# One stage for the two long convolutions of a layer, the short convolution inside its linear, and filter spectra over even and odd tokens

## What is computed

```python
def hyena_filter_spectra(z, window, w1, b1, w2, b2, w3, b3, freq):
    ...                                   # a small network of the position gives h
    h = (h @ c(w3) + c(b3)).reshape(L, HY_ORDER, 2, HY_WIDTH) * window[:, None, None, :]
    fwd, bwd = h[:, :, 0], h[:, :, 1]
    f = jnp.concatenate([fwd, zeros, bwd[1:][::-1]], axis=0)
    f = f / (jnp.sum(jnp.abs(f), axis=0, keepdims=True) + EPS)
    return jnp.fft.rfft(f, axis=0)

def hyena_mixer(u, conv_w, spec, skip):
    u = short_conv(u, conv_w)             # three taps over tokens, 1536 channels
    v, x1, x2 = jnp.split(u, 3, axis=-1)
    z = x1 * long_conv(v, spec[:, 0], skip[0])
    return x2 * long_conv(z, spec[:, 1], skip[1])
```

## Time and profile before

| | us |
|---|---|
| median of three runs | 3400.32 |
| lowest, highest | 3399.54, 3415.02 |
| the profiled execution | 3400.13 |
| its span in the trace | 3398.3 |
| TensorE busy | 2941.6 (87%) |
| VectorE busy | 2106.3 (62%) |
| ScalarE busy | 1482.0 (44%) |
| mean granted TensorE clock, share of full speed | 0.913 |

### The profile page before, as it was taken

The page is one execution under the profiler, slowest core; times in us unless marked ns, Lnnn a source line. Parts: engine busy times, 40 slices in busy tenths (PEclk is TensorE's granted clock), DMA queues, the critical chain, the costliest instruction groups (busy, mean ns, idle before and its releaser), DMA issues. The chain is left out here.

```text
span 3398.3 us, 44680 instructions
## 1 busy us (share of the span) xinstructions
PE 2941.6 (87%) x18175; PEld 2619.8 (77%) x18175; DVE 2106.3 (62%) x2152; ACT 1482.0 (44%) x1353; POOL 40.0 (1%) x65
## 2 busy tenths in 40 slices
PE   5999974699999999999967696898999686899899
PEld 4799973578888888888843584898899584899898
DVE  5555557378888888888846453555555454555554
ACT  3443432156766776676622023343434023343432
POOL 0000000000000000000000000000000000000000
PEclk8899986689999999999979886899999886899999
DMA  5255520089999999999941240344355230354352
GB/s 164 73 178 184 161 88 1 0 300 347 363 333 347 363 333 344 365 333 342 367 135 75 64 124 13 121 165 132 104 185 164 75 113 25 112 161 137 100 186 100
DMA packets 364966, 618.36 MB, mean 182 GB/s; under 512 B 16670, under 2 KB 201092, under 8 KB 363536
## 3 DMA queue, kind: packets, MB, share of 16 engines
q1 hardware_dynamic: 363656, 610.87, 52.3%
q10 hardware_dynamic: 1162, 5.36, 0.4%
HBM read 610.94 MB, written 5.24 MB: 181 GB/s over the span
## 5 line engine op out<-in xcount | busy, mean ns | idle before, releaser
L345 DVE TENSOR_TENSOR slots_low<-slots,w_hi 128x2048 fp32r<-128x2048 f32 (+2 forms) x241 | 542.1, 2253 | 579.7 <-ACT w_hi L334 579.7
L334 ACT ACTIVATE w_hi<-slots 128x2048 fp32r<-128x2048 f32 (+2 forms) x241 | 451.7, 1878 | 585.0 <-PE ps L426 263.1
L1166 DVE TENSOR_TENSOR slots_low<-slots,w_hi 128x2048 fp32r<-128x2048 f32 x224 | 504.0, 2285 | 70.7 <-ACT w_hi L1118 70.7
L426 PE MATMUL ps<-x_hi,w_hi 128*128 128x256 f32 x1488 | 438.3, 295 | 120.1 <-DVE x_lo L497 40.1
L426 PE MATMUL ps<-x_lo,w_hi 128*128 128x256 f32 x1488 | 432.9, 291 | 0.0
L426 PE MATMUL ps<-x_hi,slots_low 128*128 128x256 f32 x1488 | 432.4, 291 | 0.0
L1118 ACT ACTIVATE w_hi<-slots 128x2048 fp32r<-128x2048 f32 x224 | 415.8, 1908 | 1.1 <-DMA slots<-in_moe_w_up_dram 1.0
L426 PEld LDWEIGHTS ps<-x_hi,w_hi 128*128 128x128 f32 x1488 | 298.2, 200 | 126.5 <-issue 89.9
L1050 PE MATMUL ps<-slots_low,x_hi 128*128 128x512 f32 x896 | 349.6, 390 | 0.0
L426 PEld LDWEIGHTS ps<-x_lo,w_hi 128*128 128x128 f32 x1488 | 298.4, 201 | 0.5
L426 PEld LDWEIGHTS ps<-x_hi,slots_low 128*128 128x128 f32 x1488 | 297.8, 200 | 0.0
(11 more groups left out here) (517 smaller groups left out, 5782.9 us busy)
## 6 DMA issues: line engine op xcount, KB each, us to landing
slots<-in_moe_w_gate_dram SPq DMA_DIRECT2D x112, 1024.0 KB, 5.1
slots<-in_moe_w_up_dram SPq DMA_DIRECT2D x112, 1024.0 KB, 5.2
slots<-in_moe_w_down_dram SPq DMA_DIRECT2D x112, 1024.0 KB, 4.9
slots<-in_mlp_w_dram SPq DMA_DIRECT2D x64, 1024.0 KB, 5.3
slots<-in_w_in_dram SPq DMA_DIRECT2D x54, 1024.0 KB, 5.3
slots<-in_ffn_w_gate_dram SPq DMA_DIRECT2D x14, 1024.0 KB, 5.0
slots<-in_ffn_w_up_dram SPq DMA_DIRECT2D x14, 1024.0 KB, 5.0
slots<-in_ffn_w_down_dram SPq DMA_DIRECT2D x14, 1024.0 KB, 4.9
```

Source lines behind the costliest of these rows:

```text
L334: act.activation(w_hi[:, s.buffer, 0:s.kt * s.cols], slots[:, s.slot, 0:s.kt * s.cols], ACT.Copy).then_inc(w_hi_done, 1)
L345: dve.tensor_tensor(slots_low[:, s.slot, 0:n], slots[:, s.slot, 0:n], w_hi[:, s.buffer, 0:n].bitcast(F32), ALU.subtract).then_inc(w_lo_don ...
L426: mm = pe.matmul(b[:, t * T:(t + 1) * T], w, xx[:, k, :], **flags)
L1166: dve.tensor_tensor(low[i % NS], raw[i % NS], his[i % R].bitcast(F32), ALU.subtract).then_inc(lo_done, 1)
```

## The change

Three places are changed.

- **Short convolution.** The stage of its own is gone. Functions hung on the linear's hooks compute the taps of slab j-2 at step j, and those of slabs 4 and 5 at step 6, the last: the first tap on ScalarE (two instructions per slab), the other two on VectorE (four per slab).
- **Long convolutions.** One stage holds both. Tokens are taken as even and odd ones, as the new layout of the `dft` constant demands; the upper frequency half is stored in falling order. VectorE starts multiplying as soon as the first of the four forward results is there, GpSimd combines each part as soon as its two factors are, and TensorE transforms back part by part, accumulating in four banks at once. Skip and gate follow per m, and the second convolution turns tile m when it is done.
- **Spectra.** Filters are made for even and odd tokens. One product instead of two gives each of four half results, and GpSimd, in `join`, forms the spectra of both halves as their sums and differences. The sizes are computed from the sum p and the difference q of the filters, as max(|p|, |q|): |p| on ScalarE, |q| and the maximum on VectorE. The order of VectorE is now `size(i)`, `window(i+1)`, `scale(i)`, `store(i)`, `mix(i+1)`. ScalarE waits for the joined spectra of unit i before it sends them and goes on to unit i+1.

```diff
-    c["hy_window"] = np.ascontiguousarray(win.reshape(TT, P, 512).transpose(1, 0, 2)).reshape(P, -1)
-    k = np.arange(T)
+    c["hy_window"] = np.ascontiguousarray(win.reshape(P, TT, 512)).reshape(P, -1)
+    k = np.concatenate([i, T - 1 - i])
...
-    c["dft"] = np.ascontiguousarray(cs.reshape(2, TT, P, T).transpose(2, 1, 0, 3)).astype(np.float32).reshape(P, -1)
+    c["dft"] = np.ascontiguousarray(cs.reshape(2, P, TT, T).transpose(1, 2, 0, 3)).astype(np.float32).reshape(P, -1)
...
@@ spectra, tensor @@
-                                    pe.matmul(bank(2 * d + t), h2[:, l, t * P:(t + 1) * P], w3s[l][...],
+                                    pe.matmul(bank(2 * d + t), h2[:, l, t:T:2], w3s[l][...],
...
                         def transform(i, n):
-                            s, k = n // 2, n % 2
-                            for t in range(TT):
-                                mm = pe.matmul(bank(4 + n), dft[:, t, s, k * P:(k + 1) * P], pq[:, s, t, :], start=(t == 0), stop=(t == TT - 1))
-                            mm.then_inc(transformed, 1)
+                            s, t = n // 2, n % 2
+                            pe.matmul(bank(4 + n), dft[:, t, s, 0:P], pq[:, s, t, :], start=True, stop=True).then_inc(transformed, 1)
                         make(0)
                         for i in range(N):
-                            pe.wait_ge(absd, 2 * i + 2)
-                            if i:
-                                pe.wait_ge(outed, 4 * i)
-                            for n in range(4):
-                                mm = pe.matmul(bank(4), ones[:, :], ab[:, n // 2, n % 2, :], start=(n == 0), stop=(n == 3))
-                            mm.then_inc(summed, 1)
                             if i + 1 < N:
                                 make(i + 1)
                             pe.wait_ge(mixed, 2 * i + 2)
+                            if i:
+                                pe.wait_ge(outed, 4 * i)
                             for n in (1, 2, 3):
                                 transform(i, n)
+                            pe.wait_ge(added, i + 1)
+                            for t in range(TT):
+                                mm = pe.matmul(bank(4), ones[:, :], ab[:, t, :], start=(t == 0), stop=(t == TT - 1))
+                            mm.then_inc(summed, 1)
                             pe.wait_ge(shifted, i + 1)
                             transform(i, 0)
@@ spectra, vector @@
+                        def size(i):
+                            dve.wait_ge(mixed, 2 * i + 2)
+                            dve.scalar_tensor_tensor(out=flat(fb[:, 1]), in0=flat(pq[:, 1]), scalar=-1.0, in1=flat(pq[:, 1]),
+                                                     op0=ALU.mult, op1=ALU.max).then_inc(absd, 1)
+                            if i:
+                                dve.wait_ge(summed, i)
+                            dve.wait_ge(absd, 2 * i + 2)
+                            dve.tensor_tensor(flat(ab[:, :, :]), flat(fb[:, 0]), flat(fb[:, 1]), ALU.max).then_inc(added, 1)
...
-                                dve.tensor_tensor(F[:, k, :], bank(4 + k), sc[:, :], ALU.mult).then_inc(outed, 1)
+                                dve.tensor_tensor(halves[:, k, :], bank(4 + k), sc[:, :], ALU.mult).then_inc(outed, 1)
...
                         for i in range(N):
-                            scale(i)
+                            size(i)
                             if i + 1 < N:
                                 window(i + 1)
+                            scale(i)
                             store(i)
                             if i + 1 < N:
                                 mix(i + 1)
@@ spectra, scalar and gpsimd @@
-                            for d in range(2):
-                                act.activation(flat(ab[:, d]), flat(fb[:, d]), ACT.Abs).then_inc(absd, 1)
-                            act.wait_ge(outed, 4 * i + 4)
+                            act.wait_ge(mixed, 2 * i + 2)
+                            act.activation(flat(fb[:, 0]), flat(pq[:, 0]), ACT.Abs).then_inc(absd, 1)
+                            act.wait_ge(joined, 4 * i + 4)
                             act.dma_start(spectra_dram[l][o], flat(F[:, :, :])).then_inc(spectra_out, 16)
+                        def join(i):
+                            if i:
+                                pool.wait_ge(spectra_out, 16 * i)
+                            for n, (a, b, op) in enumerate(((2, 3, ALU.add), (3, 2, ALU.subtract), (0, 1, ALU.add), (0, 1, ALU.subtract))):
+                                pool.wait_ge(outed, 4 * i + (3 if n < 2 else 4))
+                                pool.tensor_tensor(F[:, (2, 3, 0, 1)[n], :], halves[:, a, :], halves[:, b, :], op).then_inc(joined, 1)
@@ hyena, tensor: one stage, o = 0 and 1 @@
+                        for m in range(4):
+                            if o:
+                                pe.wait_ge(outed, m + 1)
+                            for t in range(TT):
+                                mm = pe.transpose(turn_bank(o, t)[:, m * P:(m + 1) * P], src[o][:, m, t:T:2], eye[:, :])
+                        mm.then_inc(turned, 1)
+                        pe.wait_ge(act_out, o + 1)
+                        pe.wait_ge(dve_out, o + 1)
+                        for n in (0, 2, 1, 3):
+                            for t in range(TT):
+                                mm = pe.matmul(bank(n), dft[:, t, n // 2, n % 2 * P:(n % 2 + 1) * P], u[:, t, :], start=(t == 0), stop=(t == TT - 1))
+                            mm.then_inc(transformed, 1)
+                        for i, n in enumerate((0, 2, 1, 3)):
+                            pe.wait_ge(product, 4 * o + i + 1)
                             for m in range(4):
-                                for n in range(4):
-                                    mm = pe.matmul(bank(4 + m)[:, 0:T], y[:, n, m * P:(m + 1) * P], idft[:, n // 2, n % 2, :], start=(n == 0), stop=(n == 3))
+                                mm = pe.matmul(bank(4 + m)[:, 0:T], y[:, n, m * P:(m + 1) * P], idft[:, n // 2, n % 2, :], start=(i == 0), stop=(i == 3))
+                                if i == 3:
+                                    mm.then_inc(back, 1)
@@ hyena, vector @@
                             for k in range(2):
+                            dve.wait_ge(transformed, 4 * o + 2 * k + 1)
                             dve.tensor_tensor(y[:, k, :], Ak, Fc, ALU.mult).then_inc(first_, 1)
                             dve.tensor_tensor(y[:, 2 + k, :], Ak, Fs, ALU.mult).then_inc(first_, 1)
+                            dve.wait_ge(transformed, 4 * o + 2 * k + 2)
                             dve.tensor_tensor(t2[:, k, :], Bk, Fs, ALU.mult).then_inc(second_, 1)
                             dve.tensor_tensor(t2[:, 2 + k, :], Bk, Fc, ALU.mult).then_inc(second_, 1)
@@ layer @@
+                        def first_tap(*slabs):      # on ScalarE, two instructions a slab
+                            ...
+                                    act.wait_ge(more["emptied"], j + 1)
+                                    for k in (2 * j, 2 * j + 1):
+                                        act.activation(hc[:, k, :], hy[:, k, 0:T], ACT.Copy, scale=hconv(0, k)).then_inc(more["first_tap"], 1)
+                        def other_taps(*slabs):     # on VectorE, four instructions a slab
+                            ...
+                        for j in range(2, 7):
+                            slabs = (j - 2,) if j < 6 else (4, 5)
+                            hooks["act", j] = first_tap(*slabs)
+                            hooks["dve", j] = other_taps(*slabs)
```

More of the change, by code:

```diff
@@ L1424, in spectra @@
                 N = len(U)
[L1425 to L1426 removed]
+                with stage("made", "windowed", "lag0", "mixed", "absd", "added", "summed", "shifted", "inverted", "transformed", "out", "joined") as \
+                        (block, made, windowed, lag0, mixed, absd, added, summed, shifted, inverted, transformed, outed, joined):
                     @block.tensor
@@ L1521, in hyena @@
             idft = K["idft"][:, :].rearrange("p (s k t) -> p s k t", s=2, k=TT)
-            with ExitStack() as c:
+            slabs = take(2)
+            with ExitStack() as c, stage("turned", "act_out", "dve_out", "transformed", "first", "second", "product", "back", "skipped", "out") as \
+                    (block, turned, act_out, dve_out, transformed, first_, second_, product, back, skipped, outed):
                 u = sb(c, "tokens", [P, TT, 512])
```

148 lines of the change are left out of this document (79 added, 69 removed).

## The result

The changed kernel took **3361.2 us** (median of four, 3358.93 to 3363.55) against 3407.67 for the kernel before beside it (3399.54 to 3418.27): a ratio of 0.986, 95% interval 0.983 to 0.988. The forecast was 3351 in a range of 3336 to 3366. The profiled execution after has a span of 3361.7 us, that of before 3398.3: 36.6 us less, where the sum had said 49.2. The four runs of before fall into two pairs, 3399.5 and 3400.3 against 3415.0 and 3418.3; their median lies between the pairs, where no run is.

What follows compares the result with a forecast made beforehand. PE was busy 87% of the span, so time could be won only where it waits. Two layers' short (9.9) and long (20.9) convolutions save 61.7 us, spectra lose 12.5: 49.2 off 3400.1 gives 3351 us, range 3336 to 3366.

Steps and rivals of the forecast that it cites:

- Short convolution: Hyena branch: taps move into the linear, transposes start at 1900.5 instead of 1910.4, 9.9 us saved a layer.
- Long convolutions: Hyena branch: 38.8 us from first transpose to next linear instead of 59.75, 20.9 us saved a layer.
- the sum: Whole kernel: 61.7 us won in two layers' Hyena branches less 12.5 lost in the spectra, 49.2 us saved.
- The cover of the linear: Hyena linear: four slabs' taps cost nothing beside PE's work; without that cover 1.6 us a slab.
- The wait of 7.7 us: Long convolutions: PE's wait between forward and backward transform, 7.7 us, goes to zero and PE bounds.
- The clock's dip: First long convolution: 4.9 us of the forward transform run at half speed, so it takes 9.3 us.
- First pass of the spectra: Spectra stage: mix(1) starts at 1793.3, where it started at 1793.73; no gain.
- A later pass: Spectra stage: a pass takes 18.85 us instead of 17.3, as GpSimd's joins lose 1.8 us beside DVE.
- The last part: End of the spectra, after the last maximum: late sums, scale, store and joins take 14.6 us.
- That half: Spectra: GpSimd loses half its time beside two-input DVE instructions, so joins lose 1.8 of 3.6 us.
- The rival of whole exclusion: Spectra: rival (a), GpSimd and DVE exclude each other wholly, 17.9 us lost, 3356 us; chance 0.20.
- The baseline: Whole kernel: savings taken off the profiled execution's 3400.1 us, held to be the median (3400.32) within 0.3.

Runs made afterwards that it cites:

- the second execution of before: The kernel before, without an edit, run and traced once more against its own first trace: 3414.93 us.
- the last group: Runs on one chip: old spectra with zeros (3347.3 us), both gaps filled (3356.1), all that helped together (3345.7), changed kernel unchanged (3361.2); before beside them 3412.4.

## Why the prediction was right, and where it was off

The sign and the range were right, the centre was 10 us low. Of the 12.6 us that are missing between the two traces, 9.6 were in no term of the sum: they are the clock's, in code that nobody touched. That they left the time inside the range is luck; the range had been drawn for other reasons. It is luck, too, that the medians differ by 46.5 us, near the 49.2 of the sum: the median of before beside the changed kernel lies between its short and its long executions. Step by step:

- **Short convolution**, 9.9 us a layer: right. From the last eviction to the transposes 3.62 us against 3.7 forecast, and 10.1 us when undone. The cover of the linear held.
- **Long convolutions**, 38.8 us each layer: 39.75 and 39.28. The wait of 7.7 us went to zero as the sum said, and PE bounds the way back at 7.07 us (6.9 + latency). The clock's dip was placed rightly: 9.45 us from the start of the first forward transform to the transform back for 9.3. The missing 1.0 us is spread over all terms, the largest 0.4 between the convolutions (1940.31 to 1944.14, 3.83 us for 3.45). Both branches together gave 59.8 us of the 61.7.
- **First pass of the spectra**, no gain: right within 1 us. `mix(1)` starts 26.2 us after the first filter, where I had 27.1 and the kernel before 27.6.
- **A later pass**, 18.85 us: 20.05. The path was the one named: the joins stretched beside DVE's two-input instructions, ScalarE's |p| behind its send, DVE behind |p|. The size of one term failed. I let the joins lose 1.8 us; they lost 2.95 (7.87 for 4.92). From the start of `mix` to the end of the maximum it takes 10.26 us, for 9.2 forecast and 11.0 in the rival. The last part was shorter than forecast (13.2 us from the last maximum to the send for 14.6). In all 13.65 us were lost for 12.5.
- **That half came from a row read wrongly.** The window of the earlier trace rows counts three GpSimd instructions beside DVE, and I took them as three done in 2.53 us. Timeline of POOL there:

```profile
2083.33 1.30 POOL L1258 TENSOR_SCALAR decay_log<-decay_sum,total 128x64 f32<-128x64 f32 x1
2084.61 1.27 POOL L1258 TENSOR_SCALAR decay_log<-decay_sum,total 128x64 f32<-128x64 f32 x1
```

  The first of the three had begun at 2082.92, before DVE did, and took its usual 0.44 us. From 2083.33 to 2085.88 GpSimd got through two where six would fit: it lost two thirds, not half. By that the joins lose 2.4 us and a pass takes 19.45, an estimate from these rows.
- **The rival of whole exclusion was the mechanism.** Asked in windows so narrow that each holds one instruction of an engine, the timelines of POOL and DVE after show the joins and `mix` one by one:

```profile
1798.40 1.26 POOL L1530 TENSOR_TENSOR spectra<-even_odd 128x512 f32<-128x512 f32 x1 [40.15 <-DVE even_odd L1501]
1798.83 1.91 DVE L1476 TENSOR_TENSOR combined<-filters 128x1024 f32<-128x1024 f32 x1
1799.62 2.24 POOL L1530 TENSOR_TENSOR spectra<-even_odd 128x512 f32<-128x512 f32 x1
1800.66 2.28 DVE L1476 TENSOR_TENSOR combined<-filters 128x1024 f32<-128x1024 f32 x1
1801.82 2.24 POOL L1530 TENSOR_TENSOR spectra<-even_odd 128x512 f32<-128x512 f32 x1
...
1804.02 2.24 POOL L1530 TENSOR_TENSOR spectra<-even_odd 128x512 f32<-128x512 f32 x1
```

  The first join isn't slowed at all (1.26 us), though the first `mix` stands beside it for 0.83 of them; the `mix` that came second is the one that is late. Then the ends alternate: join 1799.66, `mix` 1800.74, join 1801.86, `mix` 1802.94, join 1804.06, |q| 1805.14, join 1806.26. The steps are 1.08 us for each instruction of DVE and 1.12 for each join. So each waits until the other engine's instruction is through and then runs at about its own speed; the 2.24 us of a join are one step of DVE and one of its own. Two engines that share evenly would slow the first join too. In the kernel with `mix` from PSUM it is the same: three joins at 1.26 or 1.27 us, then |q| (ends 1802.86) and the last join (2.24 us, ends 1803.97) in turn.
  The Trainium skill ("SBUF — State Buffer", Who interferes with whom) calls it an exclusive lock on ports that the two share. This trace agrees. The rival's price was too high, since it added whole durations (`mix` and |q|, 3.6 us, on top of the joins); in turn, a join's step is 2.20 us for 1.22, and three such steps lose 2.95 us. In the earlier trace rows it was not one for one: each of the two GpSimd instructions ended only after two of DVE's, which kept their pace (0.68 to 0.72 us). What decides who comes next, no run here shows.
- **The baseline** was the largest miss, and it is in no term of the change. I took the profiled execution of before for the kernel's time because it was the median of the runs shown. It was one of the short ones. The profiled execution of the changed kernel loses 6.5 us of it upstream (5.6 and 0.9) in code that nobody touched, as the second execution of before does. The changed kernel traced once more loses 4.4, and two of its variants none, so this part goes by the execution.
- **Rest of layer 1**, 3.1 us longer after (663.2 for 660.1): the difference arises within 30 us, 70 us behind the long convolutions. Windows of 5 us there, the changed kernel, then before:

```profile
2775.30:2780.30 5.00, 5.00 (x15) 2.67 (x13) 2.31 (x9) 3.28 (x10) 0.00 (x0) 0.50 0.00 0
2780.30:2785.30 5.00, 5.00 (x13) 2.63 (x12) 1.54 (x5) 2.12 (x7) 0.00 (x0) 0.50 0.00 0
```

```profile
2815.00:2820.00 5.00, 5.00 (x16) 2.67 (x16) 2.26 (x9) 3.75 (x11) 0.00 (x0) 0.66 0.01 2
2820.00:2825.00 5.00, 5.00 (x25) 2.97 (x24) 3.09 (x10) 3.22 (x11) 0.00 (x0) 1.00 0.00 0
```

  The same work gets the low clock for longer. The eleven other traces with the change's long convolutions have 662.6 to 664.5 us for this stretch, the second execution of before 660.15. Why it meets every one of them wasn't tried; the cause stays open.

Sum: 49.2 forecast, less 6.5 upstream, 1.2 spectra, 1.9 branches and 3.1 in the rest of layer 1 makes 36.5; the spans give 36.6.

Against the kernel before in its long executions the change is worth more than in the traces I compared: there the old spectra stage takes 88.5 us. The new one, whose passes are led by DVE, ACT and GpSimd, took 94.1 to 95.2 us in all six traces that have it, on whichever side the execution fell. So it costs 5.6 us or a little more then, not 13.65, and the medians beside the last group differ by 51.2 us (3412.4 less 3361.2).

What stays open: the old spectra with fillers (80.3 us) and both gaps of the long convolutions filled weren't run together. From the stretches it would be near 3347.3 less 2 x 2.8, some 3342 us, an estimate.

## What to carry to other kernels

When several waits on one engine are replaced by work that flows part by part, price the new flow by the durations of each engine between two parts; here that sum was right within 1 us of 39. Work moved to GpSimd beside VectorE instructions with two SBUF inputs costs both engines: they took turns, instruction by instruction, so count both lengths as one. A VectorE instruction that read one input from PSUM was free of it, and the joins on the busy VectorE (2.5 us for four) were cheaper than on the idle GpSimd (a stage of 87.3 us for 94.1). Where a window counts instructions, look at their starts and ends before a pace is read from it. And before a trace is taken as the baseline, compare it with a second execution of the same kernel: here gaps of TensorE of 3.3 us cost nothing in one and 1.5 to 3.1 us each in the next.

## What the runs showed of the hardware that I had not expected

- One gap of 3.32 us before the same 8 instructions left the granted clock at 1.00 in one execution and took it to 0.50 in another: 3.70 against 6.68 us, 8.1 us for the stage.
- Work that nobody reads gives this back: 14 matmuls of zeros a pass brought the stage from 88.5 to 80.3 us. In the long convolutions a filled gap handed the dip on to the next one (8.80 for 7.11 us), which had held before; only both together took the convolutions from 39.75 to 36.48 us.
- Where VectorE reads two inputs in SBUF and GpSimd reads SBUF too, they take turns by whole instructions: the first join 1.26 us, as if alone, then ends in turn every 1.08 and 1.12 us. In sum four joins take 7.87 us for 4.92, `mix` 4.11 for 2.35, |q| 2.17 for 1.22.
- A float32 scalar_tensor_tensor of 128x1024 with both inputs in SBUF (the same tile twice) takes 1.22 us, as a tensor_tensor of that size does, and filters made with weights of every second token take 3.60 us for eight, as with adjacent ones.
